# A chunked gated delta rule on one core: blocks broadcast in two halves of rows, the scaling of o behind the coefficients, other banks for X, S q's scaling inside the substitution

## The chip, the cores and the metric

One core of one Trainium2 chip runs the whole program. The metric is the device time of one execution in microseconds (us). The engines are PE (TensorE), DVE (VectorE), ACT (ScalarE), POOL (GpSimd) and SP (SyncE, which issues most DMAs). Each runs its own list of instructions in order and waits on semaphores.

## The reference, cut to what matters

One layer of a streaming encoder: a projection, a gated-DeltaNet group of 8 heads (width 128), a latent attention group, an output projection. Only the delta rule is touched by the change. Per head and chunk (128 tokens in the kernel, whatever the reference's own block) it computes:

```python
lmat = where(strict, (k*beta) k^T * decay, 0)
tmat = inverse(I + lmat)
v_new = tmat (v*beta) - tmat (k*beta*exp(g)) s
o = (q*exp(g)) s + (q k^T * decay) v_new
s = s*exp(g_last) + (k*exp(g_last-g))^T v_new
...
o_g = rmsnorm(o, gdn_norm_w) * silu(z_g)
```

The keys and queries are normalised to unit length first, and s is carried from chunk to chunk. There are 9 chunks: 8 of the prompt and one of 32 rows for the sample stream.

## The kernel before, in words

The program runs four stages one after another: `project`, `delta_rule`, `attend` (after the latents) and `project_out`. The change touches `delta_rule` alone. This stage is written out by hand as a software pipeline of *slots*: `each_slot` calls, on each engine, `slot(c)` for c = -2 to 9. In slot c three chunks are at work: chunk c (the state's step), chunk c+1 (the inverse) and chunk c+2 (norms, decays, lmat). The order of the work on an engine is the order of the calls in its `slot`. The ledgers PE, DVE, ACTS and POOL count finished steps by name, and `wait(engine, c, name)` waits for one. Each step over 8 heads is done in two halves g = 0, 1 of 4 heads, 512 columns of one PSUM bank each.

The steps and names, with their lines:

- PE per slot, in order: kS (S^T k), qT and kT (transposes of chunk c+2), qS (S^T q), y, D (log decays), G (k k^T of c+2), dS (the change of the state, "k'y"), Ay (attention part of o), oT (o of c-1 transposed), then for c+1: X, P4, Y4, X4, P5, vT, Y5, X5, A, P6, aT, Y6 (the inverse from 16-row blocks up to 128 rows). Line 981 is the matmuls of `heads`, 987 the transposes of `turn`.
- PSUM banks: 8 banks are 4 pairs. `lay_out` deals the steps of `PHASES` to the pairs in turn; a step that gets a pair waits (`free`) until the step that had it before was read, by the instruction that `FREED` names (dS by DVE's S, G by DVE's L, qS by DVE's qe). The list deals the banks only; the order in which PE runs the steps is that of its `slot`.
- DVE: `substitute` (lines 884, 886) solves the eight 16-row diagonal blocks by forward substitution: for each row i = 1 to 15 a multiply m_i of `Lrep`'s row i with the rows of x so far, and a sum x_i. R (line 903) stands after row 7, `norms` (sse, line 852) after row 13. After row 15 come qe (line 915, qS scaled by exp(g) into o), `coefficients` (kb, nlam, nle, sqc, sq2, lines 856 to 863, on 128x8 values), S (922), o (926), L (874, lmat of c+2), mix (935), the adds Y4, X4, var, Y5, X5, aI and orr.
- POOL: rs (line 687, sse to the power -1/2, chunk c+2), `on` (line 692, o of c-1 scaled by orr, 128x1024), C5 (673), gmh and gml (678), Sd (703), mix_lo (706), orms (709), C4 (673).
- ACT: squares (740), kd (731), y, dL (783), expand Yx (727, after x15), dLb (793, dL scaled by nlam), X, P4, osq, mix_hi, P5 and so on.
- SP, `bounce` (lines 636 to 646): when L of chunk c+2 is done it sends the eight diagonal blocks to DRAM (line 642, eight DMAs), waits for them, and reads them back broadcast (line 645) into `Lrep`: 128 partitions of 16 rows x 8 heads x 16, 1 MB. The DMA's shape is 8 blocks by 16 copies by 2048 numbers. In the next slot `substitute` waits for it at row 1.

Of the kernel before, what the change touches and what calls it, by code (L numbers as in the profile page):

```python
# [17 lines left out]
HEADS = 8  # L18
# [492 lines left out]
BASE = 16  # L511
NB = P // BASE
# [8 lines left out]
def delta_rule(nc, a, d, cols, ident, out, g_all, g_hi, g_lo, beta, eg, egl, edl):  # L521
# [4 lines left out]
    with ExitStack() as ctx:  # L526
        s = Space(nc, ctx, "gdn")
# [22 lines left out]
        kb, nle, sqc, sq2 = (s.sb(n, CH) for n in ("kb", "nle", "sqc", "sq2"))  # L550
# [22 lines left out]
            s.sem(n) for n in ("consts_in", "set_up", "rounded", "sample_padded", "ssm_out"))  # L573
        qkv_in = [s.sem(f"qkv_in{u}") for u in range(3)]
        gate_in, mix_out = ([s.sem(f"{n}{u}") for u in range(2)] for n in ("gate_in", "mix_out"))
        blocks_out, blocks_in = s.sem("blocks_out"), s.sem("blocks_in")
        block = ctx.enter_context(nc.Block())
        qkv_d = d["qkv"].rearrange("f p n -> p f n")
        gate_d = d["gate"].rearrange("(j z) p n -> z p j n", z=2)[0]
# [1 line left out]
        blocks_d = d["blocks"]  # L581
# [7 lines left out]
                slot(c, lambda k: 0 <= k < CHUNKS)  # L589

        PAIRS = 4
        PHASES = ["kS", "qT", "kT", "qS", "y", "D", "G", "dS", "Ay", "oT", "X", "P4_", "Y4_", "X4_", "P5_", "vT", "Y5_", "X5_", "A", "P6", "aT", "Y6"]
        LAG = {"qT": 2, "kT": 2, "D": 2, "G": 2, "kS": 0, "qS": 0, "y": 0, "dS": 0, "Ay": 0, "oT": -1}
        FREED = {"qT": (ACTS, "sqq"), "kT": (ACTS, "kd"), "D": (ACTS, "dL"), "G": (DVE, "L"), "X": (ACTS, "X"), "P4_": (ACTS, "P4_"),
                 "Y4_": (DVE, "Y4_"), "X4_": (DVE, "X4_"), "P5_": (ACTS, "P5_"), "Y5_": (DVE, "Y5_"), "X5_": (DVE, "X5_"),
# [15 lines left out]
        def at(phase, c, g):  # L611
            return 2 * place[phase, c][0] + g

        @block.sync
        def _(sp):
            for dst, src in ((upper, "upper"), (lower, "lower"), (neg, "neg"), (level, "level"), (onehot, "onehot"), (member, "member")):
                sp.dma_start(dst[:], a[src]).then_inc(consts_in, 16)
            sp.dma_start(prod[:], a["preset"][:, None, :].to_broadcast([P, HEADS, WIDE])).then_inc(consts_in, 16)
            sp.dma_start(S[:, 1], a["state_gdn_ssm"][0, 0].rearrange("h k v -> k h v")).then_inc(consts_in, 16)

            def load(c):
                n = width(c)
# [12 lines left out]
            def bounce(c):

                DVE.wait(sp, c, "L1")
                if c >= 2:
                    sp.wait_ge(blocks_in, 16 * (c - 1))
                for b in range(NB):  # L640
                    rows = slice(BASE * b, BASE * b + BASE)
                    sp.dma_start(blocks_d[c % 2, b], lmat[rows, c % 2, :, rows]).then_inc(blocks_out, 16)
                sp.wait_ge(blocks_out, 16 * NB * (c + 1))
                DVE.wait(sp, c - 1, f"m{BASE - 1}")
                sp.dma_start(Lrep[:], blocks_d[c % 2].rearrange("b i h k -> b (i h k)")[:, None, :]
                             .to_broadcast([NB, BASE, BASE * HEADS * BASE])).then_inc(blocks_in, 16)

            def slot(c, live):
                if c == -2:
                    load(0)  # L650
                    load(1)
                if live(c + 3) and c + 3 >= 2:
                    load(c + 3)
                if live(c + 2):
                    bounce(c + 2)
                if live(c + 1):
                    load_gate(c + 1)

            each_slot(slot)

        @block.gpsimd
        def _(pool):
            pool.memset(mhalf[:], -0.5).then_inc(set_up, 1)
            pool.memset(S[:, 0], 0.0).then_inc(set_up, 1)
            pool.wait_ge(set_up, 2)
            pool.wait_ge(consts_in, 16 * CONSTS)

            def mask(c, k, name, C):

                if k == 0:  # L670
# [12 lines left out]

            def slot(c, live):
                if live(c + 2):
                    DVE.wait(pool, c + 2, "sse")
                    POOL.done(pool.tensor_tensor(rs[:], sse[:], mhalf[:], ALU.pow), c + 2, "rs")
                if live(c - 1):
                    DVE.wait(pool, c - 1, "orr")
                    if live(c + 1):  # L690
                        DVE.wait(pool, c + 1, f"x{BASE - 1}")
                    POOL.done(pool.tensor_tensor(o[:, (c - 1) % 2], o[:, (c - 1) % 2], orr[:, :, None].to_broadcast(full), ALU.mult), c - 1, "on")
                if live(c + 1):
                    mask(c + 1, 1, "C5", C5)
                if live(c + 3):
                    both(c + 3)
                if c + 3 == LAST:

                    PE.wait(pool, LAST - 3, "qS1")
                    pool.memset(qkv[:, LAST % 3, :, DEC:], 0.0).then_inc(sample_padded, 1)  # L700
                if live(c + 1):
                    DVE.wait(pool, c, "S1")
                    POOL.done(pool.tensor_tensor(Sd[:], S[:, stream(c + 1)], egl[:, c + 1, :, None].to_broadcast(full), ALU.mult), c + 1, "Sd")
                if live(c - 1):
                    ACTS.wait(pool, c - 1, "mix_hi")
                    POOL.done(pool.tensor_tensor(mix_lo[:, (c - 1) % 2], mix[:], mix_hi[:, (c - 1) % 2].bitcast(F32), ALU.subtract), c - 1, "mix_lo")
                if live(c):
                    DVE.wait(pool, c, "var")
                    POOL.done(pool.tensor_tensor(orr[:], var[:], mhalf[:, 0:HEADS], ALU.pow), c, "orms")
                if live(c + 2):  # L710
                    mask(c + 2, 0, "C4", C4)

            both(0)
            each_slot(slot)
# [120 lines left out]
        def _(dve):  # L835
# [40 lines left out]
            def substitute(c, rows):  # L876

                for i in rows:
                    if i == 1:
                        dve.wait_ge(blocks_in, 16 * (c + 1))  # L880
                        ACTS.wait(dve, c - 1, "Yx")
                    else:
                        own(c, f"x{i - 1}")
                    DVE.done(dve.tensor_tensor(prod[:, :, AT[i]:AT[i] + i], Lrep[:, i, :, 0:i], x[:, :, 0:i], ALU.mult), c, f"m{i}")
                    own(c, f"m{i}")
                    DVE.done(dve.tensor_reduce(x[:, :, i:i + 1].rearrange("p h o -> p (h o)"), prod[:, :, AT[i]:AT[i] + i + 1], AX.X, ALU.add), c, f"x{i}")
# [7 lines left out]
            def slot(c, live):  # L894
# [8 lines left out]
                            last = dve.scalar_tensor_tensor(R[:, c % 2, k], bank(at("kS", c, g))[:, h], nle[:, c, k:k + 1], R[:, c % 2, k], ALU.mult, ALU.add)  # L903
                        DVE.done(last, c, f"R{g}")
                if live(c + 1):
                    substitute(c + 1, range(BASE // 2, BASE - 2))
                if live(c + 2):
                    norms(c + 2)
                if live(c + 1):
                    substitute(c + 1, range(BASE - 2, BASE))  # L910
                if live(c):
                    PE.wait(dve, c - 2, "oT1")
                    for g in G2:
                        PE.wait(dve, c, f"qS{g}")
# [1214 lines left out]
```

## Time and profile before

| what | value |
|---|---|
| time before, median of 3 runs | 2594.51 us (2593.32 to 2595.74) |
| the profiled execution's own time | 2596.67 us |
| its span in the trace | 2594.9 us |
| PE busy, share of the span | 2348.9 us, 91% |
| DVE, ACT, POOL busy | 1103.4, 747.9, 463.2 us |
| the delta rule's stage in the trace | about 1194 to 1637 us |

The profile is of one execution. Its busy shares are over the whole program; the delta rule is 443 us of it, and there PE is busy less (windows of one slot show 34 to 36 of 43 or 44 us). A timeline row gives the start, the time it took, the engine, the line, the operation, output<-input and, in brackets, how long the engine sat idle before it and what ended that.

### The profile page before, as it was taken

The numbers are of one execution on the slowest core, as the hardware profiler recorded it, in microseconds if no ns is written. First come the engines' busy times: TensorE is split into PE (matmuls) and PEld (weight loads), VectorE is DVE, ScalarE is ACT, GpSimd is POOL, SyncE is SP. The second block draws the span as 40 slices with busy tenths as digits, with TensorE's granted clock in tenths as the row PEclk, the third lists the DMA queues.
The fourth block names the chain that finished last, engine by engine and source line by source line (L and its number), as shares of the span: only waits on it lengthen the run. The fifth ranks groups of instructions, "written<-read, shape, count | busy, mean of one in ns | idle before, by whom it ended". The sixth has DMA issues, their size and how long they took to land. (4 is left out here: it accounts for less than half of the span.)

```text
span 2594.9 us, 37040 instructions
## 1 busy us (share of the span) xinstructions
PE 2348.9 (91%) x15280; PEld 2253.8 (87%) x15280; DVE 1103.4 (43%) x1743; ACT 747.9 (29%) x1860; POOL 463.2 (18%) x287
## 2 busy tenths in 40 slices
PE   6899999999999999994687878598999995999997
PEld 5899999999999999994577878497888875999997
DVE  3321354555554111111567776463544442334343
ACT  4111111111111111113355554323434332333343
POOL 0111121222222111112334443110000000111111
PEclk8999999999999999997789899798999997999999
DMA  4222122222222222213434432533222217758564
GB/s 159 70 74 74 50 75 75 74 63 69 66 74 74 74 75 74 68 48 93 79 72 111 86 71 61 171 124 105 68 58 82 63 42 244 245 145 252 150 184 129
DMA packets 328557, 257.72 MB, mean 99 GB/s; under 512 B 32533, under 2 KB 308326, under 8 KB 323942
## 3 DMA queue, kind: packets, MB, share of 16 engines
q1 hardware_dynamic: 300582, 219.33, 30.3%
q10 hardware_dynamic: 27808, 36.03, 3.8%
q8 instruction: 122, 2.00, 0.3%
q14 instruction: 45, 0.37, 0.0%
HBM read 192.42 MB, written 62.91 MB: 98 GB/s over the span
## 5 line engine op out<-in xcount | busy, mean ns | idle before, releaser
L457 PE MATMUL proj_acc<-proj_hn_hi,proj_w_hi 128*128 128x352 f32 (+1 forms) x2352 | 762.5, 324 | 7.0 <-DVE proj_hn_lo L338 6.1
L457 PE MATMUL proj_acc<-proj_hn_lo,proj_w_hi 128*128 128x352 f32 (+1 forms) x2352 | 754.9, 321 | 0.0
L457 PE MATMUL proj_acc<-proj_hn_hi,proj_w_lo 128*128 128x352 f32 (+1 forms) x2352 | 754.7, 321 | 0.0
L457 PEld LDWEIGHTS proj_acc<-proj_hn_hi,proj_w_hi 128*128 128x128 f32 (+1 forms) x2352 | 439.9, 187 | 8.7 <-issue 6.7
L457 PEld LDWEIGHTS proj_acc<-proj_hn_lo,proj_w_hi 128*128 128x128 f32 (+1 forms) x2352 | 440.8, 187 | 0.6
L457 PEld LDWEIGHTS proj_acc<-proj_hn_hi,proj_w_lo 128*128 128x128 f32 (+1 forms) x2352 | 439.6, 187 | 0.8
L2063 PE MATMUL mixo_acc<-mixo_m_hi,mixo_w_hi 128*128 128x384 f32 (+1 forms) x768 | 253.9, 331 | 30.8 <-DMA mixo_m_lo<-scratch_mix 20.9
L218 POOL TENSOR_TENSOR proj_w_raw<-proj_w_raw,all_cols 128x2048 f32<-128x2048 f32 (+1 forms) x49 | 175.6, 3584 | 418.9 <-DMA proj_w_raw<-in_w_in 418.9
L2063 PE MATMUL mixo_acc<-mixo_m_hi,mixo_w_lo 128*128 128x384 f32 (+1 forms) x768 | 249.2, 325 | 0.0
L2063 PE MATMUL mixo_acc<-mixo_m_lo,mixo_w_hi 128*128 128x384 f32 (+1 forms) x768 | 249.2, 324 | 0.0
L369 DVE TENSOR_TENSOR proj_act_out<-proj_acc,proj_rstd_b 128x352 f32<-128x352 f32 (+1 forms) x75 | 39.1, 524 | 364.5 <-PE proj_acc L457 353.4
L2001 DVE TENSOR_TENSOR mixo_w_lo<-mixo_w_raw,mixo_w_hi 128x2048 fp32r<-128x2048 f32 x48 | 110.0, 2293 | 175.2 <-ACT mixo_w_hi L1967 175.2
L343 DVE TENSOR_TENSOR proj_w_lo<-proj_w_raw,proj_w_hi 128x2048 fp32r<-128x2048 f32 (+1 forms) x49 | 111.5, 2276 | 161.7 <-ACT proj_w_hi L264 161.7
L2063 PEld LDWEIGHTS mixo_acc<-mixo_m_hi,mixo_w_hi 128*128 128x128 f32 x768 | 146.3, 190 | 33.4 <-DVE mixo_w_lo L2001 27.0
L380 DVE SCALAR_TENSOR_TENSOR proj_act_out<-proj_pre,all_cols,proj_act_out 128x1059 f32<-128x1059 f32 x72 | 172.7, 2399 | 2.5
L287 ACT ACTIVATE proj_act_out<-proj_act_out 128x1059 f32<-128x1059 f32 x24 | 26.1, 1089 | 474.6 <-DVE proj_act_out L380 474.6
L2063 PEld LDWEIGHTS mixo_acc<-mixo_m_lo,mixo_w_hi 128*128 128x128 f32 x768 | 146.5, 191 | 0.0
L2063 PEld LDWEIGHTS mixo_acc<-mixo_m_hi,mixo_w_lo 128*128 128x128 f32 x768 | 146.2, 190 | 0.0
L264 ACT CAST proj_w_hi<-proj_w_raw 128x2048 fp32r<-128x2048 f32 (+1 forms) x49 | 92.9, 1895 | 124.2 <-DVE proj_act_out L369 94.2
L365 DVE TENSOR_TENSOR proj_pre<-proj_acc,proj_rstd_b 128x352 f32<-128x352 f32 (+1 forms) x96 | 39.1, 429 | 182.4 <-PE proj_acc L457 179.9
L291 ACT ACTIVATE proj_act_out<-proj_act_out 128x1056 f32<-128x1056 f32 x16 | 17.4, 1087 | 305.0 <-DVE proj_act_out L369 305.0
L1967 ACT CAST mixo_w_hi<-mixo_w_raw 128x2048 fp32r<-128x2048 f32 x48 | 90.9, 1894 | 32.0 <-DMA mixo_w_raw<-in_w_out 32.0
(285 smaller groups left out, 3631.5 us busy)
## 6 DMA issues: line engine op xcount, KB each, us to landing
proj_w_raw<-in_w_in SPq DMA_DIRECT2D x48, 1024.0 KB, 5.7
mixo_w_raw<-in_w_out SPq DMA_DIRECT2D x48, 1024.0 KB, 6.1
scratch_qkv<-proj_act_out ACTq DMA_DIRECT2D x24, 529.5 KB, 2.8
gdn_qkv<-scratch_qkv SPq DMA_DIRECT2D x8, 1536.0 KB, 8.3
gdn_Lrep<-scratch_blocks SPq DMA_DIRECT2D x9, 1024.0 KB
scratch_gate<-proj_act_out ACTq DMA_DIRECT2D x16, 528.0 KB, 2.7
mixo_y<-in_x_prompt SPq DMA_DIRECT2D x8, 1024.0 KB, 8.8
out_y_prompt<-mixo_y SPq DMA_DIRECT2D x8, 1024.0 KB, 5.2
```

The costliest lines, as they stand in the source:

```text
L218: POOL.done(pool.tensor_tensor(w_raw[:, :, 0:n], w_raw[:, :, 0:n], cols[:, 0, R_LN:R_LN + KT][:, :, None].to_broadcast([P, KT, n]), ALU.mu ...
L264: ACTS.done(act.copy(w_hi[:, t % 2, :, 0:n], w_raw[:, :, 0:n]), t, "hi")
L287: ACTS.done(act.activation(act_out[:, b], act_out[:, b], ACT.Silu), j, "silu")
L291: ACTS.done(act.activation(act_out[:, b, 0:T], act_out[:, b, 0:T], ACT.Silu), QKV_TILES + j, "silu")
L343: DVE.done(dve.tensor_tensor(w_lo[:, t % 2, :, 0:n], w_raw[:, :, 0:n], w_hi[:, t % 2, :, 0:n].bitcast(F32), ALU.subtract), t, "lo")
L365: last = dve.tensor_tensor(pre[:, b, first + shift:end + shift], acc[b][c][:, first - NW * c:end - NW * c], rstd_b[:, first:end], ALU.mult)
L369: last = dve.tensor_tensor(act_out[0:n, b, cut(c)], acc[b][c][0:n, 0:NW], rstd_b[0:n, cut(c)], ALU.mult)
L380: DVE.done(dve.scalar_tensor_tensor(y, pre[:, b, n:n + CONV], w[n], y, ALU.mult, ALU.add), j, f"c{n}")
L457: last = pe.matmul(acc[b][c][0:n, 0:NW], w[:, b, k, 0:n], h[:, k, cut(c)], start=(k == 0 and i == 0), stop=(k == KT - 1 and i == 2))
L1967: ACTS.done(act.copy(w_hi[:, i % 2], w_raw[:, i % 2]), i, "hi")
L2001: DVE.done(dve.tensor_tensor(w_lo[:, i % 2], w_raw[:, i % 2], w_hi[:, i % 2].bitcast(F32), ALU.subtract), i, "lo")
L2063: last = pe.matmul(acc[i % 4][:, 0:n], w[:, i % 2, k], h[:, g % 2, k, 0:n], start=(k == 0 and x == 0), stop=(k == KT - 1 and x == 2))
```

## The change

Five edits, all in `delta_rule`:

1. `bounce` reads the blocks back in two DMAs of half the rows each (rows 0 to 7, rows 8 to 15), each with a semaphore of its own; `substitute` waits for the first at row 1 and for the second at row 8.
2. POOL's `on` also waits for DVE's sq2 of chunk c+2, the last of the coefficients, where there is a chunk c+2 (slots 1 to 6; in slots -1 and 0 there is no `on`).
3. In `PHASES` dS is dealt before G, so dS gets the pair that kT had, G the one that qS had, X the one that dS had, and P4 the one that G had.
4. qe moves from after row 15 to after row 10.
5. `norms` (sse) moves from after row 13 to after row 10 and qe.

```diff
-        blocks_out, blocks_in = s.sem("blocks_out"), s.sem("blocks_in")
+        blocks_out, blocks_in = s.sem("blocks_out"), [s.sem(f"blocks_in{u}") for u in range(2)]
...
-        PHASES = ["kS", "qT", "kT", "qS", "y", "D", "G", "dS", "Ay", "oT", "X", "P4_", "Y4_", "X4_", "P5_", "vT", "Y5_", "X5_", "A", "P6", "aT", "Y6"]
+        PHASES = ["kS", "qT", "kT", "qS", "y", "D", "dS", "G", "Ay", "oT", "X", "P4_", "Y4_", "X4_", "P5_", "vT", "Y5_", "X5_", "A", "P6", "aT", "Y6"]
...
                 if c >= 2:
-                    sp.wait_ge(blocks_in, 16 * (c - 1))
+                    sp.wait_ge(blocks_in[1], 16 * (c - 1))
...
-                sp.dma_start(Lrep[:], blocks_d[c % 2].rearrange("b i h k -> b (i h k)")[:, None, :]
-                             .to_broadcast([NB, BASE, BASE * HEADS * BASE])).then_inc(blocks_in, 16)
+                n = BASE // 2
+                for u in range(2):
+                    rows = slice(n * u, n * u + n)
+                    sp.dma_start(Lrep[:, rows], blocks_d[c % 2, :, rows].rearrange("b i h k -> b (i h k)")[:, None, :]
+                                 .to_broadcast([NB, BASE, n * HEADS * BASE])).then_inc(blocks_in[u], 16)
...
                     if live(c + 1):
                         DVE.wait(pool, c + 1, f"x{BASE - 1}")
+                    if live(c + 2):
+                        DVE.wait(pool, c + 2, "sq2")
                     POOL.done(pool.tensor_tensor(o[:, (c - 1) % 2], o[:, (c - 1) % 2], orr[:, :, None].to_broadcast(full), ALU.mult), c - 1, "on")
...
                 for i in rows:
+                    if i % (BASE // 2) == (1 if i < BASE // 2 else 0):
+                        dve.wait_ge(blocks_in[2 * i // BASE], 16 * (c + 1))
                     if i == 1:
-                        dve.wait_ge(blocks_in, 16 * (c + 1))
                         ACTS.wait(dve, c - 1, "Yx")
...
                 if live(c + 1):
-                    substitute(c + 1, range(BASE // 2, BASE - 2))
+                    substitute(c + 1, range(BASE // 2, BASE // 2 + 3))
+                if live(c):
+                    PE.wait(dve, c - 2, "oT1")
+                    for g in G2:
+                        PE.wait(dve, c, f"qS{g}")
+                        DVE.done(dve.tensor_tensor(o[:, c % 2, half(g)], bank(at("qS", c, g)), wide(eg, c, g), ALU.mult), c, f"qe{g}")
                 if live(c + 2):
                     norms(c + 2)
                 if live(c + 1):
-                    substitute(c + 1, range(BASE - 2, BASE))
-                if live(c):
-                    PE.wait(dve, c - 2, "oT1")
...
+                    substitute(c + 1, range(BASE // 2 + 3, BASE))
                 if live(c + 2):
                     coefficients(c + 2)
```

On DVE, between row 13 of the substitution and the coefficients, a slot stands so before (m_i is the multiply into gdn_prod, x_i the sum; 128x8x14 is row 14; L915 is qe, L852 sse, L856 kb):

```order
L884 TENSOR_TENSOR gdn_prod<-gdn_Lrep,gdn_x 128x8x13 [waits gdn_dve_base]
L886 TENSOR_REDUCE gdn_x<-gdn_prod 128x8 [waits gdn_dve_base]
L852 TENSOR_SCALAR gdn_sse<-gdn_ssq 128x16 [waits gdn_act_early]
L884 TENSOR_TENSOR gdn_prod<-gdn_Lrep,gdn_x 128x8x14 [waits gdn_dve_base]
L886 TENSOR_REDUCE gdn_x<-gdn_prod 128x8 [waits gdn_dve_base]
L884 TENSOR_TENSOR gdn_prod<-gdn_Lrep,gdn_x 128x8x15 [waits gdn_dve_base]
L886 TENSOR_REDUCE gdn_x<-gdn_prod 128x8 [waits gdn_dve_base]
L915 TENSOR_TENSOR gdn_o<-gdn_b0,gates_eg 128x512 [waits gdn_pe_state]
L915 TENSOR_TENSOR gdn_o<-gdn_b1,gates_eg 128x512 [waits gdn_pe_state]
L856 TENSOR_TENSOR gdn_kb<-gdn_rs,gates_beta 128x8 [waits gdn_pool_early]
```

Changed, from row 8 (now with the wait for the second half) on:

```order
L890 TENSOR_TENSOR gdn_prod<-gdn_Lrep,gdn_x 128x8x8 [waits gdn_dve_base,gdn_blocks_in1]
L892 TENSOR_REDUCE gdn_x<-gdn_prod 128x8 [waits gdn_dve_base]
L890 TENSOR_TENSOR gdn_prod<-gdn_Lrep,gdn_x 128x8x9 [waits gdn_dve_base]
L892 TENSOR_REDUCE gdn_x<-gdn_prod 128x8 [waits gdn_dve_base]
L890 TENSOR_TENSOR gdn_prod<-gdn_Lrep,gdn_x 128x8x10 [waits gdn_dve_base]
L892 TENSOR_REDUCE gdn_x<-gdn_prod 128x8 [waits gdn_dve_base]
L917 TENSOR_TENSOR gdn_o<-gdn_b0,gates_eg 128x512 [waits gdn_pe_state]
L917 TENSOR_TENSOR gdn_o<-gdn_b1,gates_eg 128x512 [waits gdn_pe_state]
L857 TENSOR_SCALAR gdn_sse<-gdn_ssq 128x16 [waits gdn_act_early]
L890 TENSOR_TENSOR gdn_prod<-gdn_Lrep,gdn_x 128x8x11 [waits gdn_dve_base]
```

qe and sse have moved ahead of rows 11 to 15; the coefficients now stand directly behind row 15. On PE the steps keep their order, and what moves is the bank and the wait. G, dS, X and P4 of one slot before (the first matmul of each half 0; the others repeat it):

```order
L981 MATMUL gdn_b6<-gdn_qkv 128x128 [waits gdn_act_early]
L981 MATMUL gdn_b0<-gdn_y,gdn_kd 128x128 [waits gdn_dve_state,gdn_act_early,gdn_act_state]
L981 MATMUL gdn_b2<-gdn_y,gdn_aT 128x128 [waits gdn_act_state,gdn_act_solve]
L987 MATMUL gdn_b6<-all_ident,gdn_Y 128x128 [waits gdn_dve_lmat,gdn_act_solve]
L981 MATMUL gdn_b0<-gdn_Y,gdn_C4 128x128 [waits gdn_dve_state,gdn_pool_solve]
```

and changed:

```order
L987 MATMUL gdn_b0<-gdn_qkv 128x128 [waits gdn_dve_state]
L987 MATMUL gdn_b6<-gdn_y,gdn_kd 128x128 [waits gdn_act_early,gdn_act_state]
L987 MATMUL gdn_b2<-gdn_y,gdn_aT 128x128 [waits gdn_act_state,gdn_act_solve]
L993 MATMUL gdn_b6<-all_ident,gdn_Y 128x128 [waits gdn_dve_state,gdn_act_solve]
L987 MATMUL gdn_b0<-gdn_Y,gdn_C4 128x128 [waits gdn_dve_lmat,gdn_pool_solve]
```

X waits for DVE's S instead of DVE's L, P4 for L instead of S, G for qe, and dS no longer for qe.

## Rows read from the trace of the kernel before

**Rows 1.** Timeline, PE: kS of slots 0, 1, 2, 3, 7; within slots 0, 2: Y4, dS, X.
```profile
1276.72 2.05 PE L981 MATMUL gdn_b<-gdn_S,gdn_qkv 128*128 128x128 f32 x16
...
1304.44 2.63 PE L981 MATMUL gdn_b<-gdn_pc,gdn_X 128*128 128x128 f32 x16
...
1319.97 2.05 PE L981 MATMUL gdn_b<-gdn_S,gdn_qkv 128*128 128x128 f32 x16
...
1362.71 2.05 PE L981 MATMUL gdn_b<-gdn_S,gdn_qkv 128*128 128x128 f32 x16
...
1374.60 2.02 PE L981 MATMUL gdn_b<-gdn_y,gdn_kd 128*128 128x128 f32 x16 [0.82 <-DVE gdn_o L915]
...
1386.72 1.94 PE L987 MATMUL gdn_b<-all_ident,gdn_Y 128*128 128x128 f32 x8 [7.43 <-DVE gdn_lmat L874]
...
1391.54 2.01 PE L981 MATMUL gdn_b<-gdn_pc,gdn_X 128*128 128x128 f32 x16
...
1406.46 2.05 PE L981 MATMUL gdn_b<-gdn_S,gdn_qkv 128*128 128x128 f32 x16
...
1576.98 3.84 PE L981 MATMUL gdn_b<-gdn_S,gdn_qkv 128*128 128x128 f32 x32
```

**Rows 2.** Timeline, DVE, slot 2: m1, R, m8, sse, m15, kb, nlam, L.
```profile
1364.07 0.17 DVE L884 TENSOR_TENSOR gdn_prod<-gdn_Lrep,gdn_x 128x8 f32<-128x8 f32 x1 [3.64 <-DMA gdn_Lrep<-scratch_blocks]
...
1367.17 2.15 DVE L903 SCALAR_TENSOR_TENSOR gdn_R<-gdn_b,gdn_nle,gdn_R 128x128 f32<-128x128 f32 x8
1369.24 0.22 DVE L884 TENSOR_TENSOR gdn_prod<-gdn_Lrep,gdn_x 128x64 f32<-128x64 f32 x1
...
1372.51 0.17 DVE L852 TENSOR_SCALAR gdn_sse<-gdn_ssq 128x16 f32<-128x16 f32 x1
...
1373.25 0.28 DVE L884 TENSOR_TENSOR gdn_prod<-gdn_Lrep,gdn_x 128x120 f32<-128x120 f32 x1
...
1375.70 1.85 DVE L856 TENSOR_TENSOR gdn_kb<-gdn_rs,gates_beta 128x8 f32<-128x8 f32 x1 [0.65 <-POOL gdn_rs L687]
1377.59 2.28 DVE L858 SCALAR_TENSOR_TENSOR gdn_nlam<-gdn_rs,gdn_kb 128x8 f32<-128x8 f32 x1
...
1385.89 1.28 DVE L874 TENSOR_TENSOR gdn_lmat<-gdn_b,gdn_dLb 128x512 f32<-128x512 f32 x2
```

**Rows 3.** Timeline, POOL, slot 2: rs, on, C5.
```profile
1372.75 2.91 POOL L687 TENSOR_TENSOR gdn_rs<-gdn_sse,gdn_mhalf 128x16 f32<-128x16 f32 x1 [14.24 <-DVE gdn_sse L852]
1375.64 1.89 POOL L692 TENSOR_TENSOR gdn_o<-gdn_o,gdn_orr 128x1024 f32<-128x1024 f32 x1
1377.49 2.35 POOL L673 TENSOR_TENSOR gdn_C<-gdn_lmat,gdn_level 128x1024 f32<-128x1024 f32 x1
```

**Rows 4.** Timeline, DVE: sq2 of slot -2; sse and L of slot 0.
```profile
1217.15 0.17 DVE L863 SCALAR_TENSOR_TENSOR gdn_sq<-gdn_sqc 128x8 f32<-128x8 f32 x1
...
1288.27 0.17 DVE L852 TENSOR_SCALAR gdn_sse<-gdn_ssq 128x16 f32<-128x16 f32 x1
...
1300.06 1.28 DVE L874 TENSOR_TENSOR gdn_lmat<-gdn_b,gdn_dLb 128x512 f32<-128x512 f32 x2
```

**Rows 5.** Timeline, ACT, slot 2: kd, dL, dLb.
```profile
1369.31 2.29 ACT L731 ACTIVATE gdn_kd<-gdn_b,gates_edl 128x128 f32<-128x128 f32 x8
...
1372.24 1.30 ACT L783 ACTIVATE gdn_dL<-gdn_b 128x512 f32<-128x512 f32 x2
...
1379.90 2.44 ACT L793 ACTIVATE gdn_dLb<-gdn_dL,gdn_nlam 128x128 f32<-128x128 f32 x8 [3.56 <-DVE gdn_nlam L858]
```

**Rows 6.** Timeline, SP's DMA queue: the broadcast's issue in slots 1 and 2.
```profile
1350.67 0.62 SPq L645 DMA_DIRECT2D gdn_Lrep<-scratch_blocks  x1
...
1394.29 0.62 SPq L645 DMA_DIRECT2D gdn_Lrep<-scratch_blocks  x1
```

**Rows 7.** Windows: us, PE, PEld, DVE, ACT, POOL busy, PEclk, DMA share, GB/s.
```profile
1350.60:1352.60 2.00, 2.00 (x20) 2.00 (x20) 1.65 (x3) 1.22 (x4) 0.72 (x1) 1.00 0.09 16
...
1358.60:1360.60 2.00, 2.00 (x26) 1.83 (x24) 1.46 (x3) 0.00 (x0) 0.00 (x0) 1.00 0.56 123
```

More of the change, by code:

```diff
@@ L905, in slot @@
                 if live(c + 1):
-                    substitute(c + 1, range(BASE // 2, BASE - 2))
-                if live(c + 2):
-                    norms(c + 2)
-                if live(c + 1):
-                    substitute(c + 1, range(BASE - 2, BASE))
+                    substitute(c + 1, range(BASE // 2, BASE // 2 + 3))
                 if live(c):
@@ L915, in slot @@
                         DVE.done(dve.tensor_tensor(o[:, c % 2, half(g)], bank(at("qS", c, g)), wide(eg, c, g), ALU.mult), c, f"qe{g}")
+                if live(c + 2):
+                    norms(c + 2)
+                if live(c + 1):
+                    substitute(c + 1, range(BASE // 2 + 3, BASE))
                 if live(c + 2):
```

## The prediction

> **What bounds the kernel now.** I read the page first, then the windows of the delta rule's stage, then one slot on the timelines of PE, DVE, POOL, ACT and SP, and last the windows of DMA. The page's 91% of PE is an average over stages with other limits. In this stage a slot is the time from one kS to the next: slots 1 to 6 run from 1319.97 to 1576.98, so 257.0 us or 42.8 each [rows 1]. I take slot 2 as the pattern and count from its kS at 1362.71.
>
> Three things hold it up. (a) X on PE stands idle for 7.43 us until L is done, for L is what frees its bank [rows 1]. The stretch X to Y4 then takes 4.82 us, though sixteen matmuls before the wait took 2.02. (b) L is late because the five coefficients on 128x8 values, which took 0.17 us each in slot -2 with POOL idle [rows 4], run from 1375.70 until S, o and L can follow: L starts at 1385.89, S and o before it take 1.2 each by L's own rate, so the five last 7.8 us [rows 2]. The reader is to lay POOL's rows beside them: kb runs under `on` and nlam ends when C5 does [rows 2, 3]. So a small DVE operation with both inputs in SBUF waits for POOL's large one. (c) m1 is 3.64 us late for the broadcast [rows 2], which takes 13.40 us from its issue [rows 2, 6].
>
> **The change, part by part.** Offsets (+) are counted from kS of the same slot.
>
> *Coefficients.* `on` waits for sq2, so in slots 1 to 6 POOL is idle while they run (rs ends just before kb). Five at 0.2 make 1.0 us instead of 7.8. In slots -1 and 0 there is no `on`, C5 follows rs at once, and they stay slow.
>
> *sse and qe.* sse is now at +9.80 [rows 2]. It needs kd's predecessor, the squares, which end at +6.6 [rows 5]. Then it stands behind row 10 and qe: R ends at +3.4 (kS's first half at +1.1, R takes 2.1 [rows 2]), rows 8 to 10 take 1.6 (rows 8 to 13 take 3.27 [rows 2]), qe 1.3 (two halves, as L's 1.28 [rows 2]). So sse comes at about +7, rs ends at +10.3, rows 11 to 15 (five rows at 0.6, m15 alone 0.28 [rows 2], so 3.0) end at about +10.2, and the coefficients at +11.3.
>
> *ACT sets L then.* dL ends at +10.8 [rows 5]. Yx needs x15, then dLb needs nlam; each takes 2.44 [rows 5], so dLb ends at +15.7. DVE's S and o follow PE (dS, Ay) and end at +15.5. L then ends at +16.8 instead of +24.46 (1385.89 + 1.28 - 1362.71).
>
> *Banks.* PE's order is unchanged. dS now starts at +11.9 after 0.82 us for qe's bank [rows 1]; without it at +11.1. dS and Ay take 3.65 (two groups of sixteen, a little under the 2.02 of dS [rows 1], since groups overlap), oT with eight 1.0, so X starts at +15.7 if its new releaser S (+13.7), Yx (+13.2) and `on` (+13.2, for oT) are there, and they are. P4 takes over the wait for L (half 0 at +16.1, PE there at +16.7): no stall. PE has not stood still, so X and P4 take 2.7 instead of 4.82, by the rate before the wait [rows 1]. Y4 starts at +18.4 instead of +28.83 and the next kS 14.92 later as now (1391.54 to 1406.46 [rows 1]): a slot of 33.3 us.
>
> *G* now waits for qe (+7.1 at the latest half); PE gets to G at +9. No cost; if qe were 2 us later, G would be late next.
>
> *The two halves.* The second DMA costs SP one more issue of 0.62 [rows 6], behind the first, ahead only of the gate load that is needed a slot later. Nothing is queued that waits. The issue comes 7.1 us after L (1387.17 to 1394.29 [rows 2, 6]), at +23.9. For the first half I have bounds of 6.7 us (half of 13.40) and 13.4. In the first 2 us the DMA share is 0.09, later 0.56 at 123 GB/s [rows 7], so the transfer is a start of some 1.7 us and then bytes at a rate: 1.7 + 11.7 / 2 = 7.6, nearest the lower end. It lands at +31.5, which is -1.8 before the next kS; DVE is free at -2.3 (1364.07 - 3.64). Rows 1 to 7 take 3.1 [rows 2] and end at +1.3, about when R can start. The second half lands 13.7 after the issue, at +4.3, where R ends at +3.4; sse has that slack nearly. The writes of the mixture (line 770) go out on ACT's queue at each slot's start and may hold it up by 0 to 2.2 us more; I take 0.7. So a slot is **34.0 us**, between 33.3 and 35.5.
>
> The share of 0.56 says that about half of the 16 DMA engines carry the broadcast [rows 7]. The Trainium skill, "DMA: Bandwidth & Descriptors", section "Why a DMA increments its semaphore by 16 and not by 1", says why: the outermost size, here 8, sets how many engines are used, and it is the lowest-numbered ones. By that both halves queue on the same eight. No run here shows which eight; had the second half the other eight, a slot would be 33.3.
>
> *First and last slots.* Slot -1: rows 1 to 7 (3.1) now run before the second half is in, and sse stands ahead of rows 11 to 13 (half of 3.27, 1.7): 4.8 us. Slot 0: sse comes at +11.55 now (1288.27 - 1276.72 [rows 1, 4]) and at +7.2 then, 4.35; and Y4, now 3.7 behind L's first half (1300.06 + 0.64 to 1304.44 [rows 1, 4]), follows it at once, for P4 needs only S there: 3.5. Together 7.9. Slot 7 has no coefficients, and its `on` waits for x15 as now: 0, between -2 and +1. Slot 8 and the stages after are as they were.
>
> *The sum*: 4.8 + 7.9 + (257.0 - 6 x 34.0 = 53.0) + 0 = 65.7 us. Against the profiled execution's 2596.67 that is 2531.0; the median of the runs is 2.2 lower, so I predict **2528.8 us**. With 33.3 and 35.5 a slot, and 1 more and 4 less at the ends, it is 2523 to 2542.
>
> **The rivals.**
>
> *A port held by rs.* Now m15 runs under rs and takes its 0.28 us [rows 2, 3], so rs does not stop DVE, and that is what I sum with. With the change all five multiplies of rows 11 to 15 lie under rs. Were DVE held until rs ends, x15 would come at +13.4, dLb at +18.3, Y4 at +19.6: a slot of 35.0 and 2535 us. The Trainium skill, "SBUF — State Buffer", section "Who interferes with whom", gives this rule: a DVE operation with two SBUF inputs contends with a GpSimd one that reads SBUF, for the whole instruction. It agrees with kb and nlam under `on` and C5 and differs from m15 under rs.
>
> *The halves land together.* If the packets of both mix, m1 waits 13.4 as now. From the issue round: 7.1 + 13.4, rows 1 to 7 3.1, R 2.1, rows 8 to 10 1.6, qe 1.3, rows 11 to 15 3.2, Yx and dLb 4.9, L 0.7: 37.3 a slot, a gain of 6 x 5.5 = 33 and some 6 at the start: 2555 us. For it: nothing in the trace shows two such transfers in line. Against: both go out on SP's queue, the first half 0.62 us ahead, and a queue that served them in order would land the first alone.
>
> *The coefficients are slow by themselves.* Then they end at +18.1, S, o and L at +21.8, `on` at +20.0, X at +21.1, and a slot is 38.7: 25 + 13 gained, 2557 us. Against it stands slot -2 [rows 4].
>
> *Slower: the price is by rows, not bytes.* Each half has the same 128 rows of the destination. If a half costs what the whole does, the second lands 13.4 + 11.7 = 25.1 after the issue, and row 8 waits for it in every slot: 7.1 + 25.1 and from m8 on 1.6 + 1.3 + 3.2 + 4.9 + 0.7 is 43.9 a slot, 6 us lost in six slots; slot -1 loses 7, slot 0 about 2, and in slot 7 x15 and `on` come 10 late: **2620 us**. It decides from about 22 us on. Against it: 123 GB/s is a rate of large packets, near 1 MB in 9 us.
>
> **How the numbers follow.** The forecast has 0.70, the port of rs 0.06 (inside its range), the halves together 0.10, slow coefficients 0.05, a mix of small losses that leaves 2545 to 2590 0.02, no change 0.03, slower 0.04. The range 2521 to 2556 holds the first three and leaves out about 0.14; the forecast's own is 2523 to 2542. A measurement here can tell 0.2% (5 us) from no change. Faster 0.93, same 0.03, slower 0.04.
>
> **What would show it.** Right: X's wait on L gone; kS to kS 33 to 35 us in slots 1 to 6 and no shorter in slot 7; kb to sq2 in about 1 us in slots 1 to 6 and still near 7 in slots -1 and 0; `on` behind sq2 and oT without an idle time before it; m1 with little wait and m8 with 0 to 3 us of DMA wait. Wrong: m1 waiting 5 us or more (halves together), m8 waiting 10 or more (price by rows), multiplies m11 to m15 of 1 us or more (rs holds the port), X idle for `on` or S.

## The result, and the profile after

| what | before | changed |
|---|---|---|
| median of 4 runs each, us | 2593.91 (2589.91 to 2595.74) | 2522.85 (2520.95 to 2524.59) |
| the profiled execution, us | 2596.67 | 2522.24 |
| its span, us | 2594.9 | 2520.4 |
| PE, DVE busy, us | 2348.9, 1103.4 | 2329.6, 1068.6 |

The ratio is 0.9728, 95% interval 0.9711 to 0.9745: faster by 71 us. The forecast of 2528.8 was 6 us too high; its range (2521 to 2556) holds the result.

Timeline of PE after the change: kS of slots 0, 1 and 2; dS, X and Y4 of slot 2; then kS of slots 3, 6, 7 and 8.

```profile
1267.86 2.05 PE L987 MATMUL gdn_b<-gdn_S,gdn_qkv 128*128 128x128 f32 x16
...
1304.41 2.05 PE L987 MATMUL gdn_b<-gdn_S,gdn_qkv 128*128 128x128 f32 x16
...
1336.87 2.05 PE L987 MATMUL gdn_b<-gdn_S,gdn_qkv 128*128 128x128 f32 x16
...
1347.26 1.95 PE L987 MATMUL gdn_b<-gdn_y,gdn_kd 128*128 128x128 f32 x16
...
1351.70 1.04 PE L993 MATMUL gdn_b<-all_ident,gdn_Y 128*128 128x128 f32 x8
...
1354.41 2.02 PE L987 MATMUL gdn_b<-gdn_pc,gdn_X 128*128 128x128 f32 x16
...
1369.34 2.05 PE L987 MATMUL gdn_b<-gdn_S,gdn_qkv 128*128 128x128 f32 x16
...
1466.73 2.05 PE L987 MATMUL gdn_b<-gdn_S,gdn_qkv 128*128 128x128 f32 x16
...
1504.06 3.84 PE L987 MATMUL gdn_b<-gdn_S,gdn_qkv 128*128 128x128 f32 x32
...
1533.67 3.84 PE L987 MATMUL gdn_b<-gdn_S,gdn_qkv 128*128 128x128 f32 x32
```

Of the kernel before, kS of slots 6 and 8, which stand beside [rows 1]:

```profile
1536.58 2.05 PE L981 MATMUL gdn_b<-gdn_S,gdn_qkv 128*128 128x128 f32 x16
...
1607.39 3.84 PE L981 MATMUL gdn_b<-gdn_S,gdn_qkv 128*128 128x128 f32 x32
```

Beside [rows 1], X's idle time of 7.43 us is gone, and so is the 0.82 ahead of dS. Slot 2 takes 32.47 us where it took 43.75. Every number below is a difference of such kS rows (the last row goes to the end of the span):

| stretch, us | before | changed | gain | forecast |
|---|---|---|---|---|
| span's start to kS(0) | 1276.72 | 1267.86 | 8.86 | 4.8 |
| slot 0 | 43.25 | 36.55 | 6.70 | 7.9 |
| slots 1 to 5 | 216.6 | 162.3 (32.46 each) | 54.3 | 46.6 |
| slot 6 | 40.40 | 37.33 | 3.1 | 6.4 |
| slot 7 | 30.41 | 29.61 | 0.80 | 0 |
| behind it | 987.5 | 986.7 | 0.8 | 0 |

The gains add up to 74.5, the difference of the spans; the forecast's split of slots 1 to 6 is by its flat 34.0 a slot. The project stage, which no edit touches, was 1.1 us longer in this run, so the start gained about 10.

DVE in slot 2 after the change, the rows that answer to [rows 2] (m1, which stands ahead of kS; R; m11 and m15; kb and sq2; L):

```profile
1334.95 0.18 DVE L890 TENSOR_TENSOR gdn_prod<-gdn_Lrep,gdn_x 128x8 f32<-128x8 f32 x1 [0.37 <-DMA gdn_Lrep<-scratch_blocks]
...
1338.07 2.16 DVE L909 SCALAR_TENSOR_TENSOR gdn_R<-gdn_b,gdn_nle,gdn_R 128x128 f32<-128x128 f32 x8
...
1343.82 0.25 DVE L890 TENSOR_TENSOR gdn_prod<-gdn_Lrep,gdn_x 128x88 f32<-128x88 f32 x1
...
1346.22 0.28 DVE L890 TENSOR_TENSOR gdn_prod<-gdn_Lrep,gdn_x 128x120 f32<-128x120 f32 x1
...
1346.93 0.17 DVE L861 TENSOR_TENSOR gdn_kb<-gdn_rs,gates_beta 128x8 f32<-128x8 f32 x1
...
1347.62 0.17 DVE L868 SCALAR_TENSOR_TENSOR gdn_sq<-gdn_sqc 128x8 f32<-128x8 f32 x1
...
1351.63 1.51 DVE L879 TENSOR_TENSOR gdn_lmat<-gdn_b,gdn_dLb 128x512 f32<-128x512 f32 x2
```

POOL in slot 2 beside it, as in [rows 3]: rs, then `on`.

```profile
1343.99 2.91 POOL L690 TENSOR_TENSOR gdn_rs<-gdn_sse,gdn_mhalf 128x16 f32<-128x16 f32 x1 [11.31 <-DVE gdn_sse L857]
1347.95 1.90 POOL L697 TENSOR_TENSOR gdn_o<-gdn_o,gdn_orr 128x1024 f32<-128x1024 f32 x1 [1.05 <-DVE gdn_sq L868]
```

The coefficients take 0.86 us from kb's start to sq2's end (before, 7.8), and the price is POOL's 1.05 us of idle time ahead of `on`. The multiplies m12 to m15 run wholly under rs (m11 starts 0.17 us ahead of it), and all five take 0.25 to 0.28 us; m1 waits 0.37 us instead of 3.64. Windows by slot (columns as in [rows 7]): slot 2 before, then changed.

```profile
1362.71:1406.46 43.75, 35.35 (x296) 34.07 (x294) 31.87 (x67) 24.33 (x95) 19.02 (x9) 0.92 0.44 100
```

```profile
1336.87:1369.34 32.47, 32.47 (x297) 31.74 (x295) 25.33 (x68) 24.00 (x95) 19.03 (x9) 1.00 0.56 132
```

PE is busy for all of the slot, at the full clock. So in slots 1 to 5 PE's own list of instructions is the bound now.

### The profile page after: what moved, and what is told of

It is laid out like the page before. It is cut to its first block and busy times, and to the rows that moved or that the text cites. A ratio compares the mean times of both kernels' runs of the same rounds, so it can differ in the third digit from the quotient of the medians.

```text
span 2520.4 us, 37058 instructions
## 1 busy us (share of the span) xinstructions
PE 2329.6 (92%) x15280; PEld 2238.0 (89%) x15280; DVE 1068.6 (42%) x1743; ACT 746.4 (30%) x1860; POOL 463.4 (18%) x287
```

## A wait that nobody counted: slot 6

Slot 6 takes 4.87 us longer than its neighbours. SP's DMA queue at the end of slot 5, changed kernel:

```profile
1455.32 0.36 SPq L628 DMA_DIRECT2D gdn_qkv<-scratch_qkv  x1
1455.78 7.70 SPq L642 DMA_DIRECT2D scratch_blocks<-gdn_lmat  x8
1464.75 1.27 SPq L648 DMA_DIRECT2D gdn_Lrep<-scratch_blocks  x2
```

POOL there (the memset clears the padding of the last, short chunk), and DVE at L and at the next m1:

```profile
1451.39 1.90 POOL L681 TENSOR_TENSOR gdn_gm_lo<-gdn_lower,gates_g_lo 128x1024 fp32r<-128x1024 f32 x1
1453.22 2.02 POOL L705 MEMSET gdn_qkv<- 128x2304 f32 x1
```

```profile
1449.03 1.51 DVE L879 TENSOR_TENSOR gdn_lmat<-gdn_b,gdn_dLb 128x512 f32<-128x512 f32 x2
...
1471.47 0.17 DVE L890 TENSOR_TENSOR gdn_prod<-gdn_Lrep,gdn_x 128x8 f32<-128x8 f32 x1 [7.03 <-DMA gdn_Lrep<-scratch_blocks]
```

L is done at 1450.54, but SP has a load ahead of the bounce, and this load, of the last chunk, waits for the memset, which stands on POOL behind `on`, C5 and the two growth products and ends at 1455.24. The bounce goes out 0.10 us behind the load, 5.2 us behind L. Before the change the same load went out at 1516.06, ahead of L's end at 1517.65, and cost nothing: L was as late as the memset. The forecast's sentence on SP, that nothing is queued that waits, fails here.

## The experiments

Times are medians of the runs; the ratio is to the kernel before, with its 95% interval. A first group takes one part out of the change, a second puts one part alone on the kernel before, and two more carry the change on.

| kernel | us | ratio (interval) | slots 0 to 7, kS to kS, us |
|---|---|---|---|
| changed | 2522.85 | 0.9728 (0.9711 to 0.9745) | 36.6, five of 32.5, 37.3, 29.6 |
| e1, one broadcast | 2566.53 | 0.9890 (0.9873 to 0.9906) | 42.3, 37.0 to 37.4, 44.8, 35.3 |
| e2, no wait for sq2 | 2543.43 | 0.9807 (0.9792 to 0.9821) | 37.8, 36.1 to 38.9, 34.6, 29.6 |
| e3, old banks | 2530.98 | 0.9757 (0.9743 to 0.9772) | 39.5, five of 33.6, 37.5, 29.6 |
| e4, qe and sse in old places | 2524.09 | 0.9732 (0.9717 to 0.9746) | 34.6, 36.2, four of 32.8, 38.5, 28.6 |
| a1, halves alone | 2567.27 | 0.9898 (0.9881 to 0.9914) | 39.0, 41.0 to 41.7, 37.1, 28.6 |
| a2, sq2 wait alone | 2567.61 | 0.9903 (0.9888 to 0.9918) | 43.8, 35.2 to 37.4, 45.3, 34.1 |
| a3, banks alone | 2594.62 | 1.0005 (0.9995 to 1.0015) | 38.9, 41.6 to 45.8, 38.0, 33.8 |
| b1, bounce first | 2515.83 | 0.9703 (0.9689 to 0.9718) | 35.5, five of 32.5, 33.7, 30.0 |
| b2, and the wait behind rs | 2509.43 | 0.9677 (0.9663 to 0.9690) | 32.0, five of 32.5, 33.9, 29.8 |

**e1: one broadcast again.**

```diff
-                n = BASE // 2
-                for u in range(2):
...
+                sp.dma_start(Lrep[:], blocks_d[c % 2].rearrange("b i h k -> b (i h k)")[:, None, :]
+                             .to_broadcast([NB, BASE, BASE * HEADS * BASE])).then_inc(blocks_in[1], 16)
...
-                    if i % (BASE // 2) == (1 if i < BASE // 2 else 0):
-                        dve.wait_ge(blocks_in[2 * i // BASE], 16 * (c + 1))
+                    if i == 1:
+                        dve.wait_ge(blocks_in[1], 16 * (c + 1))
```

> The changed kernel with the blocks of L broadcast in one transfer again, awaited by row 1 of the substitution. My theory: the halves let DVE start on row 1 about 7 us after the issue and not after 13.4; without them the loop of broadcast, substitution and L holds the slots again, row 1 waits about 13.4 us, a slot takes about 37.4 us where the change's takes 32.5, and the time is about 2558 us. Rival: the transfer would be hidden anyway now, since PE has no idle wait in slots 1 to 5 of the change; then 2523 to 2530 us.

Measured: 2566.53 us. Its broadcast of slot 1, and the m1 that waits for it:

```profile
1342.58 0.62 SPq L645 DMA_DIRECT2D gdn_Lrep<-scratch_blocks  x1
```

```profile
1356.02 0.17 DVE L887 TENSOR_TENSOR gdn_prod<-gdn_Lrep,gdn_x 128x8 f32<-128x8 f32 x1 [6.57 <-DMA gdn_Lrep<-scratch_blocks]
```

13.44 us from issue to m1, and 37.0 to 37.4 us a slot: the theory's mechanism and its size. The time is 8.5 us above the theory's: the load ahead of the last bounce costs more here (slot 6, at 44.8, is 7.6 over its neighbours, and 4.9 in the change), and slot 7 loses 5.6. The rival (hidden anyway) is refuted.

**e2: `on` without its wait for sq2.**

```diff
-                    if live(c + 2):
-                        DVE.wait(pool, c + 2, "sq2")
```

> The changed kernel without the wait of POOL's scaling of o for sq2. My theory: the coefficients take 7.8 us again and not 1.0, L, its bounce and S q's scaling come about 5 us later, the loop over broadcast and substitution holds the slots at about 37.6 us, and the time is 2551 to 2555 us, with the seven coefficient rows at 1.2 to 2.3 us each. Rival: X no longer waits for L in the new banks, so PE does not feel the coefficients; then about 2525 us.

Measured: 2543.43 us. DVE's kb, nlam and nle in slot 2, then PE's X and P4 there:

```profile
1350.61 0.17 DVE L859 TENSOR_TENSOR gdn_kb<-gdn_rs,gates_beta 128x8 f32<-128x8 f32 x1
1350.81 1.75 DVE L861 SCALAR_TENSOR_TENSOR gdn_nlam<-gdn_rs,gdn_kb 128x8 f32<-128x8 f32 x1
1352.59 2.29 DVE L863 TENSOR_TENSOR gdn_nle<-gdn_nlam,gates_eg 128x8 f32<-128x8 f32 x1
```

```profile
1357.49 1.16 PE L991 MATMUL gdn_b<-all_ident,gdn_Y 128*128 128x128 f32 x8 [1.92 <-DVE gdn_S L926]
1359.88 3.76 PE L985 MATMUL gdn_b<-gdn_Y,gdn_C 128*128 128x128 f32 x16 [1.23 <-DVE gdn_lmat L877]
```

The coefficients are slow again (in this slot all but kb and sqc; they are five, not the seven of the expectation). PE feels it in the new banks too, since X now waits for S, which follows the coefficients, and P4 for L. So the rival is refuted.

Slots 1 to 5 take 37.7 us on average, the theory's 37.6, but not by the loop it names: m1 waits 0.30 us for its half in slot 2 and not at all in slots 1 and 3 to 7. What lengthens a slot is PE's waits (1.9 and 1.2 us) and the granted clock behind them. In slot 1 that clock is 1.00 from X to Y4 and the slot takes 36.1; in slot 2, above, it is 0.63 and the slot takes 38.9. The number came out by luck.

The time is 8 us under the theory's lower end. 3.0 of it is slot 6: with L late again (it ends at 1475.20, the load goes out at 1475.47) the memset is hidden, and the slot takes 34.6 where 37.6 was expected. Another 3.5 lie outside the slots (kS(0) 1.3 us earlier, what follows kS(8) 2.2 shorter than in the change's run).

**e3: G and dS dealt in the old order.**

```diff
-        PHASES = ["kS", "qT", "kT", "qS", "y", "D", "dS", "G", "Ay",
+        PHASES = ["kS", "qT", "kT", "qS", "y", "D", "G", "dS", "Ay",
...
```

> The changed kernel with G and dS in their old order, so that X stands in other banks and takes the place of L's operand again. My theory: with the coefficients fast X waits only some 1.0 us per slot in slots 1 to 6 (it would start 16 us behind kS in place of 14.8), and the time is about 2529 us. Rival: the banks are the main gain, since X waited for DVE's mask by 7.4 us in a slot before; then X waits by as much again and the time is about 2567 us.

Measured: 2530.98 us. X of slot 2:

```profile
1357.10 1.35 PE L993 MATMUL gdn_b<-all_ident,gdn_Y 128*128 128x128 f32 x8 [0.60 <-DVE gdn_lmat L879]
```

X waits 0.60 us and a slot is 1.1 us longer, five times over, with 3.0 more in slot 0, where the coefficients are slow and P4 waits for L. X's 7.43 us of before was the lateness of L, not the place of X; the rival is refuted.

**e4: qe and sse in their old places.**

```diff
-                    substitute(c + 1, range(BASE // 2, BASE // 2 + 3))
-                if live(c):
-                    PE.wait(dve, c - 2, "oT1")
...
+                    substitute(c + 1, range(BASE // 2, BASE - 2))
                 if live(c + 2):
                     norms(c + 2)
                 if live(c + 1):
-                    substitute(c + 1, range(BASE // 2 + 3, BASE))
+                    substitute(c + 1, range(BASE - 2, BASE))
+                if live(c):
+                    PE.wait(dve, c - 2, "oT1")
...
```

> The changed kernel with S q's scaling and the sums of squares back in their old places on DVE, behind the whole substitution and ahead of its last two rows. My theory: the scaling is needed by oT late enough in slots 1 to 6 that its place is worth next to nothing there, and 2 to 3 us in slots -1 and 0 together; about 2525 us. Rival: PE waits for the scaling's second half at oT in every slot, 3 us each; then about 2541 us.

Measured: 2524.09 us; its interval overlaps the change's, so the whole effect can't be told from none. Inside, kS(0) comes 2.8 us later, slot 0 is 2.0 shorter, slot 1 is 3.7 longer and the four slots behind it 0.3 longer each; slot 6 is 1.2 longer and slot 7 1.1 shorter. PE waits for qe, but at G and not at oT, and in three slots only (0.24 us in slot 0, 1.82 in slot 1, 1.29 in slot 6). So the rival is refuted, and the theory is right in the total only.

**a1, a2, a3: each part alone on the kernel before.** The edits are those of the change's diff: the two half transfers (a1), the wait for sq2 (a2), the order of G and dS (a3).

> The kernel before with the two half transfers alone. My theory: m1 comes some 6.5 us earlier per slot, but the seven coefficients still take 7.8 us and L, which X waits for, follows them; a slot falls from 42.8 to about 39 us, and the time is about 2569 us. Rival: both halves come in only when the whole did, or X's wait for L alone sets the slot; then 2585 to 2595 us.

> The kernel before with the wait of POOL's scaling of o for sq2 alone. My theory: the coefficients fall from 7.8 to about 1.0 us in slots 1 to 6, L's bounce comes as much earlier, and a slot is the loop of the whole transfer and the substitution, about 37.1 us; the time is about 2560 us, the largest part of the change by itself. Rival: the coefficients' rows are slow by themselves; then 2594 us or more, as POOL's scaling comes later.

> The kernel before with X moved into the other banks alone. My theory: X no longer waits for L, but the next slot's work waits for the broadcast that comes from L's bounce all the same; 2592 to 2595 us. Rival: X's wait of about 7.4 us is on the path by itself; a slot gains at least 2.4 us and the time is 2580 us or less.

Measured: 2567.27, 2567.61 and 2594.62 us. In a1 m1 has no wait left, and X still waits for L. X and P4 of its slot 2, and the window on them:

```profile
1372.47 1.94 PE L991 MATMUL gdn_b<-all_ident,gdn_Y 128*128 128x128 f32 x8 [6.06 <-DVE gdn_lmat L877]
1374.20 3.62 PE L985 MATMUL gdn_b<-gdn_Y,gdn_C 128*128 128x128 f32 x16
```

```profile
1372.47:1377.62 5.15, 5.15 (x25) 5.15 (x25) 1.77 (x3) 1.76 (x3) 0.03 (x1) 0.50 0.10 10
```

Its slot is 32.46 of PE's work, 6.06 of waiting and 5.15 - 2.71 = 2.4 because PE runs at the granted clock 0.50 (1.2 GHz of 2.4) behind that wait: 41.0, and the rows say 41.0 to 41.7. The theory's 39 a slot left the clock out; its total is right because the ends gain more. In a2 slots 1 to 5 are quicker than expected (36.0 on average), but the load ahead of the last bounce, which waits for the memset, costs it more than the change: it goes out at 1488.94, the broadcast 8.55 us behind it, and m1 waits 12.96 us. Slots 6 and 7 take 8.6 us more than before, where the theory had slot 6 take 3.3 less: 11.9, of which the quicker slots 1 to 5 give back 5.5. That is 6.4 of the miss of 7.6 us. a3 moves nothing.

Alone the two main parts gain 26.6 and 26.3 us on the median of before in the result's table, 53 together; taken out of the change they cost 43.7 and 20.6. They stand in one loop (substitution, coefficients, L, bounce, broadcast) beside PE's list, so what one is worth depends on the other.

**b1: the last bounce ahead of the last load.**

```diff
-                if live(c + 3) and c + 3 >= 2:
+                if live(c + 3) and 2 <= c + 3 < LAST:
                     load(c + 3)
                 if live(c + 2):
                     bounce(c + 2)
+                if c + 3 == LAST:
+                    load(c + 3)
```

> The changed kernel with one change of SP's order: in slot 5 the last block's bounce and broadcast stand ahead of the load of the last chunk, which waits for POOL's memset. My theory: the bounce goes out when L is written, about 5 us earlier, row 1 of slot 6 no longer waits 7.0 us, slot 6 takes about 32.5 us in place of 37.3, and the time is about 2518 us (4 to 5 us under the change). Rival: the last chunk's load now comes later and slot 6 or 7 waits for it; then as much is given back and the time is within 2 us of the change's.

Measured: 2515.83 us, 7.0 under the change; its runs (2514.3 to 2517.0) lie below all of the change's. SP's queue at the end of slot 5:

```profile
1449.24 5.10 SPq L642 DMA_DIRECT2D scratch_blocks<-gdn_lmat  x8
1455.60 1.26 SPq L648 DMA_DIRECT2D gdn_Lrep<-scratch_blocks  x2
1456.96 0.39 SPq L628 DMA_DIRECT2D gdn_qkv<-scratch_qkv  x1
```

The bounce leaves 0.03 us behind L's end (1449.21). Slot 6 falls from 37.33 to 33.66; of the rest, 0.98 us is PE's wait for the late load in slot 6, which is all that is left of the rival. That shows the mechanism of slot 6. The profiled spans differ by 5.2 us, 3.7 of it in slot 6; the rest lies where the edit does nothing. The largest part of it, slot 0's 1.0 us, goes with the granted clock. P4 of slot 0, in the changed kernel and here:

```profile
1286.07 3.54 PE L987 MATMUL gdn_b<-gdn_Y,gdn_C 128*128 128x128 f32 x16 [3.22 <-DVE gdn_S L928]
```

```profile
1285.79 2.02 PE L989 MATMUL gdn_b<-gdn_Y,gdn_C 128*128 128x128 f32 x16 [3.23 <-DVE gdn_S L930]
```

The wait is the same; the clock up to the next product is 0.54 there and 1.00 here.

**b2: POOL waits for sq2 right behind rs.** On top of b1:

```diff
                     POOL.done(pool.tensor_tensor(rs[:], sse[:], mhalf[:], ALU.pow), c + 2, "rs")
+                    if c >= 1:
+                        DVE.wait(pool, c - 1, "orr")
+                        DVE.wait(pool, c + 1, f"x{BASE - 1}")
+                    DVE.wait(pool, c + 2, "sq2")
...
-                    if live(c + 2):
-                        DVE.wait(pool, c + 2, "sq2")
```

> The version of SP's order just run (last bounce ahead of the last load), and POOL's wait for sq2 moved from the scaling of o to the place right behind rs, so that it stands ahead of all of POOL's full-width work in every slot that computes coefficients, the three slots without a scaling of o among them (-2, -1 and 0). My theory: any of POOL's large products (C, the growth products, the scaling of o) slows the coefficients, so they become fast in those three slots too: L of slot -2 comes about 2.5 us earlier (then held by ACT), in slot 0 PE's waits of 3.23 us for S and 0.37 us for L go; some 6 us in all, about 2510 us. Rival: C and the growth products don't slow the coefficients, only the scaling of o does; then the coefficients stay at 1.8 to 2.3 us in slots -1 and 0, C comes 6 us later there, and the time is 2516 us or more.

Measured: 2509.43 us, 13.4 under the change and 0.9677 of before: the fastest version. DVE in slot 0 of the changed kernel (kb, nlam, nle):

```profile
1279.02 2.31 DVE L861 TENSOR_TENSOR gdn_kb<-gdn_rs,gates_beta 128x8 f32<-128x8 f32 x1
1281.36 1.82 DVE L863 SCALAR_TENSOR_TENSOR gdn_nlam<-gdn_rs,gdn_kb 128x8 f32<-128x8 f32 x1
1283.22 1.82 DVE L865 TENSOR_TENSOR gdn_nle<-gdn_nlam,gates_eg 128x8 f32<-128x8 f32 x1
```

The same in b2, then POOL there (rs, C):

```profile
1274.61 0.17 DVE L865 TENSOR_TENSOR gdn_kb<-gdn_rs,gates_beta 128x8 f32<-128x8 f32 x1
1274.81 0.17 DVE L867 SCALAR_TENSOR_TENSOR gdn_nlam<-gdn_rs,gdn_kb 128x8 f32<-128x8 f32 x1
1275.01 0.17 DVE L869 TENSOR_TENSOR gdn_nle<-gdn_nlam,gates_eg 128x8 f32<-128x8 f32 x1
```

```profile
1271.68 2.90 POOL L692 TENSOR_TENSOR gdn_rs<-gdn_sse,gdn_mhalf 128x16 f32<-128x16 f32 x1 [18.80 <-DVE gdn_sse L861]
1275.54 2.37 POOL L678 TENSOR_TENSOR gdn_C<-gdn_lmat,gdn_level 128x1024 f32<-128x1024 f32 x1 [0.96 <-DVE gdn_sq L872]
```

C behind the coefficients instead of beside them: kb 0.17 us instead of 2.31, and slot 0 in 31.96 us instead of 35.54 (b1). kS(0) comes 3.0 us earlier than in b1, so 6.6 of the expected 6. The rival (only `on` slows them) is refuted.

## Why the prediction was right, and where its terms were off

- **Coefficients (five in 1.0 us, slow by POOL's work beside them): right.** 0.86 us in slot 2, slow in slots -1 and 0 as said. One reading behind it was wrong: in slot -2 of the kernel before only nle, sqc and sq2 took 0.17 us; kb and nlam took 1.85 and 1.82 there, beside POOL's growth products, which fits the same cause. e2 and b2 show the cause from both sides: let POOL's product run and they are slow, hold it back and they are fast. So the rival "slow by themselves" is refuted.
- **The halves: right, 7.6 us for the first was a little high.** Slot 2's m1 follows its issue by 6.98 us (1327.97 to 1334.95), between the bounds of 6.7 and 13.4 and near the lower one. m8 never waits in the slots 1 to 5, so the 0.7 us a slot for mixture writes ahead of the second half was not there. The rivals "together" and "by rows" fall with it: 6.98 us cannot be a landing at 13.4.
- **A slot of 34.0 us: too high by 1.54.** 0.7 is the term above. The other 0.84 is in the path from kS to X: dS starts 10.39 us behind kS, forecast 11.1, and X 4.44 behind dS, forecast 4.6. X to Y4 takes 2.71 as forecast (2.7), Y4 to kS 14.93 (14.92). That is 7.7 us over slots 1 to 5. The 11.1 took only the 0.82 ahead of dS off the 11.89 of before, but y was late there too. y of slot 2, before and changed:

```profile
1368.44 2.16 PE L981 MATMUL gdn_b<-gdn_R,gdn_Y 128*128 128x128 f32 x16
```

```profile
1342.29 1.95 PE L987 MATMUL gdn_b<-gdn_R,gdn_Y 128*128 128x128 f32 x16
```

Before, y starts 5.73 us behind kS, while R, late with m1, still runs (until 1369.32 [rows 2]); changed, it starts 5.42 behind kS and R is done. That is 0.31; y to D gives another 0.21 and G to dS 0.16 beyond the 0.82. The granted clock has no part in it: from kS to dS it is 1.00 in both kernels.
- **Slot 6: 34.0 forecast, 37.33 measured.** The step "nothing is queued that waits" failed; SP's load behind POOL's memset was missed, and b1 shows it. The forecast read SP's queue in slots 1 and 2 only. There the load is out well before L, in the changed kernel too (1342.49 against 1351.63 in slot 2).
- **Slot -1: 4.8 forecast, 8.9 to 10 measured.** The sum kept the second half where the whole had landed. In slot -1 the whole took 14.54 us from issue to m1 (1226.58 to 1241.12 before; e1: 14.31), but with halves m8 started 12.41 us behind the issue: 2.1. And the sum left out the clock: before, PE stood idle for 3.09 us ahead of Y4 and ran Y4 and X4 at about half of it, so that Y4 to kS took 17.76 us, and 14.93 after the change: 2.8. The issue and m8 of slot -1, changed:

```profile
1227.68 1.31 SPq L648 DMA_DIRECT2D gdn_Lrep<-scratch_blocks  x2
```

```profile
1240.09 0.22 DVE L890 TENSOR_TENSOR gdn_prod<-gdn_Lrep,gdn_x 128x64 f32<-128x64 f32 x1 [2.55 <-DMA gdn_Lrep<-scratch_blocks]
```

Windows on the two products Y4 and X4 of slot -1, before and changed (columns as above; there the granted clock is 0.55, here 1.00):

```profile
1258.96:1265.60 6.64, 6.63 (x34) 6.64 (x35) 2.97 (x5) 0.39 (x1) 2.36 (x1) 0.55 0.10 9
```

```profile
1252.93:1258.36 5.43, 5.43 (x48) 5.43 (x49) 3.65 (x6) 0.97 (x2) 2.36 (x1) 1.00 0.08 8
```

- **Slot 0: 7.9 forecast, 6.7 measured.** sse comes at +7.98 and not at +7.2, since m1 waits 2.49 us for its half: 0.8 short. Y4 follows L's first half by 1.1 us and not at once, since P4 waits 3.22 us for S and then runs its sixteen products in 3.54 us instead of 1.95 (the clock again, 0.54 there): 0.9 short. Y4 to the next kS is 0.5 shorter, which the sum had at nothing.
- **Banks: right as a part, worth little.** P4 takes over L without a stall in slots 1 to 5, and by e3 the whole edit is worth 8 us of the 71.
- **rs on the port: refuted.** m12 to m15 under rs take 0.26 to 0.28 us. The rule of the Trainium skill, "SBUF — State Buffer", section "Who interferes with whom", would have DVE wait there. The trace differs for rs and agrees for C, the growth products and `on`, whose stretches the coefficients wait out. (The rival's 35.0 a slot doesn't follow from its own terms: Y4 at +19.6 and 14.92 make 34.5.)

The errors were -1.54 a slot five times, -4.1 at the start, +1.2 in slot 0, +3.3 in slot 6 and -1.6 behind it: 8.8 us too high on the profiled execution, the difference of 74.5 and 65.7. So the total is closer than its terms: 13.4 us of gain that the forecast missed stand against 4.5 that it counted and that did not come, and that part of the agreement is luck. The cause of the 1.6 behind slot 6 (0.8 in slot 7, 0.8 after it) is open.

## What to carry to other kernels

When a loop is shortened, list for every queue what else is in it in *each* iteration, the last ones too: a wait that was covered by the old lateness (here a load behind a memset) comes out as soon as the lateness goes. Tiny operations that wait beside another engine's large one can be freed by holding back the large one for the microsecond they need, and in every iteration, not only where it was noticed. Price parts in pairs where they stand in one loop: alone the halves gain 27 us and the wait 26, but without the halves the change would lose 44.

## What the runs showed of the hardware that was not expected

- Two half broadcasts were in sooner than the whole: 12.41 us from the first issue to m8, against 14.31 and 14.54 to m1 for the whole in the same slot (slot -1). It is so in every kernel here: 12.25 to 12.62 us in the seven with halves, 14.31 to 14.54 in the four with the whole. Why was not tried.
- POOL's rs (2.91 us, 128x16, both inputs in SBUF) does not delay DVE's multiplies of two SBUF inputs, while POOL's 128x1024 products hold up DVE's 128x8 operations by about their own 1.9 to 2.4 us. Two SBUF inputs are not needed for that: DVE's last operation on var (L898, one input tensor, 128x8) took 2.28 us in slot 5 of the change, where it began at 1457.16 beside POOL's mix_lo (1457.06 to 1459.41), and 0.17 in the slots before and after. What sets rs apart from the products was not tried.
- The same wait of PE can leave the granted clock high or low. It was 0.50 behind 6.06 us of waiting in a1 (2.4 us more) and 0.54 behind 3.22 us in slot 0 of the change (1.6 us more), but 1.00 behind 3.23 us at the same place in b1. In e2, X and P4 wait 1.9 and 1.2 us in slots 1 and 2 alike, and from X to Y4 the clock is 1.00 in slot 1 and 0.63 in slot 2. In slot 6 of the change PE stood 3.52 us for R, and the slot's mean clock is 1.00. What decides is open.
